# Looping over the feature chunks outermost in the first feed-forward step of each layer

## The chip, the cores and the metric

One core of one Trainium2 chip. The metric is the device time of one execution in microseconds (us); a kernel's time is the median of its runs. Engines run in parallel and each works through its own instructions in order: PE (TensorE, matmuls), ACT (ScalarE), DVE (VectorE), POOL (GpSimd), SP (issues the DMAs). They meet only at semaphores.

## What is computed

Two layers of a transformer-like trunk over 512 latent and 256 context tokens, width 1024. Only the feed-forward half of a layer matters here; in the second (last) layer the context tokens drop out of it.

```python
def swiglu(z, wg, wu, wd):
    return (jax.nn.silu(z @ wg) * (z @ wu)) @ wd
...
        mx = jnp.split(silu_c @ w_mod[l] + b_mod[l], 6, axis=-1)
        mc = jnp.split(silu_cc @ w_mod[l] + b_mod[l], 6, axis=-1)
...
        x = x + mx[5] * swiglu(modulate(rms_norm(x, norm2_g[l]), mx[3], mx[4]), w_gate[l], w_up[l], w_down[l])

        if not last:
...
            h = h + mc[5] * swiglu(modulate(rms_norm(h, norm2_g[l]), mc[3], mc[4]), w_gate[l], w_up[l], w_down[l])
```

The hidden width is 2816, the type is fp32 throughout.

## The kernel before

**Tiling.** Everything is kept transposed: features on the 128 partitions (8 chunks `k` of the 1024 features), tokens in the free dimension, 0 to 511 latent and 512 to 767 context. To keep fp32 precision each operand is split into a rounded part and a rest: `zh`/`zl` for the activations, `wh`/`wl` for the weights, and a product is three passes, `wh*zh + wh*zl + wl*zh`. `three_pass` (L1358) does that for one half panel: for each chunk `k`, three matmuls of 512 columns and, in layer 0, three of 256 for the context.

**The FFN.** It runs in 11 steps of 256 hidden units (`ffn_step`, L1604), each in two halves `h` of 128. A half has a gate accumulator in PSUM bank `3h`, an up accumulator in bank `3h + 1`, and both context parts in bank `3h + 2`. PE's order in a step: gate half 0, up half 0, gate half 1, up half 1, then the down projection of the step before (`down`, L1585). In layer 0 PE also computes one panel per step of layer 1's modulation row from `w_mod`: `ffn_mod(s, 0)` after up half 0 and `ffn_mod(s, 1)` after gate half 1, four matmuls for each of four quarters, from `wh_m`, `wl_m`, and then `mod_finish` (L1307) at the end of the step.

**The weights.** SP loads a panel into `raw`; ACT copies it, rounded, to `wh` (L487) as soon as the last user of that half is done (semaphores `use_a`, `use_b`, `use_m`, raised by PE); POOL subtracts to get `wl` (L382, semaphores `loA`, `loB`, `loM`, `loD`). `wh[0]` holds gate, `wh[1]` up, one panel each with two halves, `wh_m` the mod panel, `wh_d` down. ACT's order in a step: `gs` (the silu of the gate accumulator, half 0, after `use_b`), next gate half 0, next up half 0, in layer 0 two mod quarters, then `hh` (rounded hidden values, after DVE's product `hf`), and the same for half 1. POOL's order: `wl_d` x2, then for each half `wl` gate, `wl` up, `wl_m` x2. SP's order in a step of layer 0: gate, up, the two mod panels' halves (each waits for the previous `wl_m`), down (waits for the previous `wl_d`), then gate and up of the next step.

**The normalisation before the first step.** `norm(2l + 1)` makes the 8 chunks of z one after the other: DVE scales (`nxz`), ACT rounds (`zh`), POOL subtracts (`zl`; chunk 0 is DVE's). PE waits for chunk `k` by `z_wait`. After its last `zl`, POOL makes the first two `wl_m`, and ACT the two `wh_m` after its last `zh`.

**The first step before** is `ffn_step(0, 0, first=True)`: only its gate half 0 waits for the z chunks one by one.

Of the kernel before, what the change touches and what calls it, by code (L numbers as in the profile page):

```python
# [21 lines left out]
P = 128  # L22
D = 1024
KC = D // P
DEPTH = 2
SX = 512
SC = 256
# [50 lines left out]
def trunk(nc, x, c, ctx_in, c_ctx, w_mod, b_mod, norm1_g, norm2_g, w_in, ret_decay_f, ret_decay_b, ret_norm_g,  # L78
          attn_sink, cm_norm_g, cm_w_s, cm_b_s, w_out, w_gate, w_up, w_down, final_norm_g, consts, out):
    stack = ExitStack()  # L80
    with stack:
# [5 lines left out]
        def sem(name):  # L87
            if name not in sems:
                sems[name] = stack.enter_context(nc.semaphore(name))
            return sems[name]  # L90
# [14 lines left out]
        zh = sb("zh", [P, KC, NT], F32R)  # L105
        zl = sb("zl", [P, KC, NT], F32R)
        raw = [sb(f"raw{i}", [P, 2048]) for i in range(2)]
        wh = [sb(f"wh{i}", [P, 2, 1024], F32R) for i in range(2)]
        wl = [sb(f"wl{i}", [P, 2, 1024], F32R) for i in range(2)]
# [75 lines left out]
        ps = stack.enter_context(nc.psum_tensor("ps", [P, 8, 512], F32))  # L185

        def parts(l_or_w):
            return [(0, SX, 0)] + ([(SX, NT, 1)] if l_or_w else [])
# [12 lines left out]
        A_GATE = [a + 4 for a in A_OUT]  # L201
        N_MODB = 2 * NP_IN
        B_UP = [N_MODB, N_MODB + FSTEPS]

        J_IN, J_FFN = 4, 4 + NP_IN

        def z_wait(eng, u, k):

            if k in Z_DVE:
                eng.wait_ge(sem("z_dve"), len(Z_DVE) * u + Z_DVE.index(k) + 1)  # L210
            else:
                eng.wait_ge(sem("z_pool"), len(Z_POOL) * u + Z_POOL.index(k) + 1)
# [1081 lines left out]
        def _(pe):  # L1294
            MM, TR = nc.tensor.matmul, nc.tensor.transpose
# [11 lines left out]
            def mod_finish(J):  # L1307

                pe.wait_ge(sem("modrow_rdy"), J + 1)
                for i in range(4):  # L1310
                    last = MM(ps[:, MODCOLS[0], 256 + 2 * i:258 + 2 * i], modrow[0:4, P * i:P * i + P], sel, start=True, stop=True)
                last.then_inc(sem("mod_fin"), 1)
# [12 lines left out]
            for k in range(KC):  # L1325
                if k >= 2:
                    pe.wait_ge(sem("xt_evac"), k - 1)
                for t in range(6):
                    dst = ps[:, k % 2, P * t:P * t + P] if t < 4 else ps[:, 2 + k % 2, P * (t - 4):P * (t - 4) + P]
                    last = TR(dst, xin[:, t, P * k:P * k + P], eye)  # L1330
# [4 lines left out]
            for i in range(8):  # L1335
                last = TR(ps[:, 5 + i // 4, P * (i % 4):P * (i % 4) + P], cws[:, i, :], eye)
# [21 lines left out]
            def three_pass(wt_h, wt_l, h, dsts, ctx, norm_u=None):  # L1358

                for k in range(KC):  # L1360
                    w = slice(P * k, P * k + P)
                    if norm_u is not None:
                        z_wait(pe, norm_u, k)
                    for c0, c1, s in parts(ctx):
                        dst = dsts[s]
                        MM(dst, wt_h[:, h, w], zh[:, k, c0:c1], start=(k == 0), stop=False)  # L1366
                        MM(dst, wt_h[:, h, w], zl[:, k, c0:c1], start=False, stop=False)  # L1367
                        last = MM(dst, wt_l[:, h, w], zh[:, k, c0:c1], start=False, stop=(k == KC - 1))  # L1368
                return last
# [5 lines left out]
            for l in range(DEPTH):  # L1375
# [203 lines left out]
                def ffn_mod(s, h):  # L1579
                    for hh_ in range(2):  # L1580
                        pe.wait_ge(sem("loM"), 4 * s + 2 * h + hh_ + 1)
                        last = mod_half(2 * h + hh_, wh_m[:, hh_, :], wl_m[:, hh_, :])
                        last.then_inc(sem("use_m"), 1)

                def down(s, par, wd_h=wh_d, wd_l=wl_d):  # L1585
                    pe.wait_ge(sem(f"loD{l}"), 2 * s + 2)
                    pe.wait_ge(sem(f"h_rdy{l}"), 2 * s + 2)
                    start = type(s) is int and s == 0
                    for n in range(KC):
                        w = slice(P * n, P * n + P)  # L1590
                        for c0, c1, sc in parts(l == 0):

                            if sc == 0 and not (start and n == 0):
                                pe.wait_ge(sem(f"ev_d{l}"), KC * s + n)
                            if sc == 1 and not (start and n < 2):
                                pe.wait_ge(sem(f"ev_dc{l}"), KC * s + n - 1)
                            dst = ps[:, (0, 6)[n % 2], :] if sc == 0 else ps[:, (2, 7)[n % 2], 0:SC]
                            for k in range(2):
                                MM(dst, wd_h[:, k, w], hh[:, par, k, c0:c1], start=(k == 0), stop=False)  # L1599
                                MM(dst, wd_h[:, k, w], hl[:, par, k, c0:c1], start=False, stop=False)  # L1600
                                last = MM(dst, wd_l[:, k, w], hh[:, par, k, c0:c1], start=False, stop=(k == 1))  # L1601
                            last.then_inc(sem(f"dn{sc}_mm{l}"), 1)

                def ffn_step(s, par, first=False):  # L1604
                    a, b = A_GATE[l] + s, B_UP[l] + s
                    if not (type(s) is int and s < 2):

                        pe.wait_ge(sem(f"ev_d{l}"), KC * (s - 1))
                        if l == 0:
                            pe.wait_ge(sem("ev_dc0"), KC * (s - 1) - 1)  # L1610
                    for h in range(2):
                        pe.wait_ge(sem("loA"), 2 * a + h + 1)

                        pe.wait_ge(sem(f"ev_h{l}"), 2 * s + h) if not first else None
                        last = three_pass(wh[0], wl[0], h, (ps[:, 3 * h, :], ps[:, 3 * h + 2, 0:SC]), l == 0,
                                          2 * l + 1 if first and h == 0 else None)
                        last.then_inc(sem("use_a"), 1)
                        if l == 0 and h:
                            ffn_mod(s, 1)
                        pe.wait_ge(sem("loB"), 2 * (b - N_MODB) + h + 1)  # L1620
                        if l == 0 and h == 0 and not first:

                            pe.wait_ge(sem("modcol_rdy"), J_FFN + s)
                        last = three_pass(wh[1], wl[1], h, (ps[:, 3 * h + 1, :], ps[:, 3 * h + 2, SC:2 * SC]), l == 0)
                        last.then_inc(sem("use_b"), 1)
                        if l == 0 and h == 0:
                            if not first:

                                pe.wait_ge(sem("ev_d0"), KC * (s - 1) + 1)
                            ffn_mod(s, 0)  # L1630

                    pe.wait_ge(sem(f"ev_h{l}"), 2 * s + 2)
                    if l == 0:
                        mod_finish(J_FFN + s)
                    if not first:
                        down(s - 1, 1 - par)

                ffn_step(0, 0, first=True)
                ffn_step(1, 1)
                with pe.Fori(0, 4) as i:  # L1640
                    ffn_step(2 * i + 2, 0)
# [65 lines left out]
```

## Time and profile before

| | us |
|---|---|
| median of 3 runs | 2202.4 |
| lowest and highest run | 2200.58, 2208.09 |
| span of the profiled execution | 2204.4 |
| PE busy in it | 1927.6 (87%) |
| POOL busy | 665.9 (30%) |
| ACT busy | 629.6 (29%) |
| DVE busy | 874.0 (40%) |

The profiled execution lies 2.0 us above the median. The first FFN step of layer 0 runs from about 691 to 748 us of the span, that of layer 1 from about 1797 to 1829 us. In the rows further down, a time is the start from the beginning of the span, "idle before" stands in brackets with what ended it, and PEclk is the TensorE clock granted, as a share of 2.4 GHz.

### The profile page before, as it was taken

The numbers are of one execution on the slowest core, as the hardware profiler recorded it, in microseconds if no ns is written. First come the engines' busy times: TensorE is split into PE (matmuls) and PEld (weight loads), VectorE is DVE, ScalarE is ACT, GpSimd is POOL, SyncE is SP. The second block draws the span as 40 slices with busy tenths as digits, with TensorE's granted clock in tenths as the row PEclk, the third lists the DMA queues.
The fourth block names the chain that finished last, engine by engine and source line by source line (L and its number), as shares of the span: only waits on it lengthen the run. The fifth ranks groups of instructions, "written<-read, shape, count | busy, mean of one in ns | idle before, by whom it ended". The sixth has DMA issues, their size and how long they took to land.

```text
span 2204.4 us, 22301 instructions
## 1 busy us (share of the span) xinstructions
PE 1927.6 (87%) x8746; PEld 1443.3 (65%) x8746; DVE 874.0 (40%) x1238; ACT 629.6 (29%) x938; POOL 665.9 (30%) x288
## 2 busy tenths in 40 slices
PE   5589898978795989999999996987977869999997
PEld 4468772244484878888888884864134647877875
DVE  5653354255436122222222238125345352334235
ACT  6233332045413222222222212133135232212222
POOL 0521213000024444444444432233100145434440
PEclk8789995589996999999999997987579979999999
DMA  7233430000011322222222310121000131332321
GB/s 258 77 114 127 121 96 19 0 1 1 1 47 68 129 94 84 85 87 94 95 95 95 107 46 0 58 65 50 0 0 0 35 99 58 115 101 70 114 76 39
DMA packets 121902, 155.55 MB, mean 71 GB/s; under 512 B 20320, under 2 KB 89712, under 8 KB 121712
## 3 DMA queue, kind: packets, MB, share of 16 engines
q1 hardware_dynamic: 121840, 154.71, 22.2%
q8 instruction: 40, 0.66, 0.1%
q14 instruction: 22, 0.18, 0.0%
HBM read 152.60 MB, written 2.10 MB: 70 GB/s over the span
## 4 chain that ended last, share of the span: by engine, by line
PE 37%; issue 31%; DVE 12%; POOL 11%; ACT 5%; DMA 4%; SPq 1%; POOLq 0%; DVEq 0%; ACTq 0%
PE ps L1366 6%; PE ps L1367 6%; PE ps L1368 6%; POOL wl_m L382 5%; POOL wl L382 3%; PE ps L1468 3%; PE ps L1456 2%; PE ps L1599 2%; PE ps L1601 2%; PE ps L1600 2%; PE ps L1303 2%; DVE nxz L989 2%; POOL wl_d L382 2%; DVE wl L1004 1%; DMA raw<-in_w_in_dram 1%
## 5 line engine op out<-in xcount | busy, mean ns | idle before, releaser
L382 POOL TENSOR_TENSOR wl<-raw,wh 128x1024 fp32r<-128x1024 f32 x144 | 348.8, 2434 | 1200.6 <-ACT wh L487 1200.6
L1366 PE MATMUL ps<-zh,wh 128*128 128x512 f32 x1728 | 630.0, 365 | 72.9 <-DVE zl L974 38.0
L1367 PE MATMUL ps<-zl,wh 128*128 128x512 f32 x1728 | 625.1, 362 | 0.0
L1368 PE MATMUL ps<-zh,wl 128*128 128x512 f32 x1728 | 620.9, 359 | 0.0
L1366 PEld LDWEIGHTS ps<-zh,wh 128*128 128x128 f32 x1728 | 335.6, 194 | 141.2 <-issue 46.8
L1368 PEld LDWEIGHTS ps<-zh,wl 128*128 128x128 f32 x1728 | 334.5, 194 | 50.0
L1367 PEld LDWEIGHTS ps<-zl,wh 128*128 128x128 f32 x1728 | 336.0, 194 | 47.6
L487 ACT ACTIVATE wh<-raw 128x1024 fp32r<-128x1024 f32 (+1 forms) x186 | 196.3, 1086 | 420.9 <-DMA raw<-in_w_in_dram 147.9
L1254 DVE SCALAR_TENSOR_TENSOR xT<-ps,modcol,xT 128x512 f32<-128x512 f32 (+1 forms) x264 | 168.0, 661 | 97.8 <-PE ps L1601 94.3
L1235 DVE TENSOR_TENSOR hf<-gs,ps 128x512 f32<-128x512 f32 x66 | 37.6, 597 | 411.8 <-ACT gs L800 411.7
L1599 PE MATMUL ps<-hh,wh_d 128*128 128x512 f32 x480 | 173.5, 361 | 12.6 <-DVE xT L1254 12.5
L1600 PE MATMUL ps<-hl,wh_d 128*128 128x512 f32 x480 | 171.4, 357 | 0.0
L1601 PE MATMUL ps<-hh,wl_d 128*128 128x512 f32 x480 | 170.4, 355 | 0.0
L800 ACT ACTIVATE gs<-ps 128x512 f32<-128x512 f32 x44 | 26.4, 599 | 468.2 <-PE ps L1368 468.2
L1241 DVE TENSOR_TENSOR hl<-hf,hh 128x768 fp32r<-128x768 f32 (+1 forms) x44 | 92.5, 2102 | 124.0 <-ACT hh L487 124.0
L382 POOL TENSOR_TENSOR wl_d<-raw_d,wh_d 128x1024 fp32r<-128x1024 f32 x40 | 95.1, 2399 | 127.4 <-ACT wh_d L487 127.4
L382 POOL TENSOR_TENSOR wl_m<-raw_m,wh_m 128x1024 fp32r<-128x1024 f32 x44 | 119.4, 2732 | 0.0
L1468 PE MATMUL ps<-Pm,vtok 128*64 128x512 f32 (+1 forms) x112 | 100.9, 1011 | 12.1 <-DVE Pm L1116 12.1
L1599 PEld LDWEIGHTS ps<-hh,wh_d 128*128 128x128 f32 x480 | 91.1, 190 | 30.5 <-DVE xT L1254 16.9
L1456 PE MATMUL ps<-rq,rk 64*128 64x512 f32 (+1 forms) x112 | 102.7, 1022 | 0.0
L1601 PEld LDWEIGHTS ps<-hh,wl_d 128*128 128x128 f32 x480 | 90.8, 189 | 13.6
L1600 PEld LDWEIGHTS ps<-hl,wh_d 128*128 128x128 f32 x480 | 91.2, 190 | 12.5
(204 smaller groups left out, 2095.0 us busy)
## 6 DMA issues: line engine op xcount, KB each, us to landing
raw<-in_w_mod_dram SPq DMA_DIRECT2D x24, 1024.0 KB, 5.3
raw<-in_w_gate_dram SPq DMA_DIRECT2D x22, 1024.0 KB, 7.1
raw<-in_w_up_dram SPq DMA_DIRECT2D x22, 1024.0 KB, 9.5
raw_m<-in_w_mod_dram SPq DMA_DIRECT2D x22, 1024.0 KB, 5.2
raw_d<-in_w_down_dram SPq DMA_DIRECT2D x20, 1024.0 KB, 5.1
raw<-in_w_in_dram SPq DMA_DIRECT2D x14, 1024.0 KB, 6.8
raw<-in_w_out_dram SPq DMA_DIRECT2D x32, 256.0 KB, 4.4
raw<-in_w_in_dram SPq DMA_DIRECT2D x16, 256.0 KB, 4.6
```

Of the source, the lines that this page charges most:

```text
L382: nc.gpsimd.tensor_tensor(dst, src, hi.bitcast(F32), ALU.subtract).then_inc(sem(done), 1)
L487: return nc.scalar.activation(dst, src, ACT.Copy)
L1241: V.tensor_tensor(hl[:, par, h, 0:W], hf[:, 0:W], hh[:, par, h, 0:W].bitcast(F32), ALU.subtract).then_inc(sem(f"h_rdy{l}"), 1)
L1254: last = V.scalar_tensor_tensor(xT[:, n, c0:c1], src, modcol[:, 48 * l + 40 + n, sc:sc + 1], xT[:, n, c0:c1], ALU.mult, ALU.add)
L1366: MM(dst, wt_h[:, h, w], zh[:, k, c0:c1], start=(k == 0), stop=False)
L1367: MM(dst, wt_h[:, h, w], zl[:, k, c0:c1], start=False, stop=False)
L1368: last = MM(dst, wt_l[:, h, w], zh[:, k, c0:c1], start=False, stop=(k == KC - 1))
L1456: MM(ps[:, j % 3, 0:q.stop - q.start], rk[b:b + 64, r, P * c:P * c + P], rq[b:b + 64, r, q], start=True, stop=True).then_inc(sem(f"ret_sc{ ...
L1468: last = MM(ps[b:b + 64, 5 + s, 0:n], vtok[:, c, HD * h:HD * h + HD], Pm[:, j % 3, 0:n], start=first, stop=(c == 5))
L1599: MM(dst, wd_h[:, k, w], hh[:, par, k, c0:c1], start=(k == 0), stop=False)
L1600: MM(dst, wd_h[:, k, w], hl[:, par, k, c0:c1], start=False, stop=False)
L1601: last = MM(dst, wd_l[:, k, w], hh[:, par, k, c0:c1], start=False, stop=(k == 1))
```

## The change

`ffn_first` replaces `ffn_step(0, 0, first=True)`. Its outer loop runs over the chunks `k`; inside it, halves and gate or up; four accumulators (with the context six regions) are open at once. The context parts of gate and up share a bank, so only the first matmul into it has the start flag. The semaphores `use_a` and `use_b` are raised by the last chunk only. Both parts of mod panel 0 leave the middle of the step: `ffn_mod(0, 0)` stands ahead of the loop, `ffn_mod(0, 1)` behind it. ACT, DVE, POOL and SP keep their code.

```diff
--- before.py
+++ after.py
@@ -1601,7 +1601,35 @@
                                 last = MM(dst, wd_l[:, k, w], hh[:, par, k, c0:c1], start=False, stop=(k == 1))
                             last.then_inc(sem(f"dn{sc}_mm{l}"), 1)
 
-                def ffn_step(s, par, first=False):
+                def ffn_first():
+
+                    a, b = A_GATE[l], B_UP[l]
+                    if l == 0:
+                        ffn_mod(0, 0)
+                    pe.wait_ge(sem("loA"), 2 * a + 2)
+                    pe.wait_ge(sem("loB"), 2 * (b - N_MODB) + 2)
+                    for k in range(KC):
+                        w = slice(P * k, P * k + P)
+                        z_wait(pe, 2 * l + 1, k)
+                        for h in range(2):
+                            for up in range(2):
+                                wt_h, wt_l = wh[up][:, h, w], wl[up][:, h, w]
+                                for c0, c1, sc in parts(l == 0):
+                                    dst = ps[:, 3 * h + up, :] if sc == 0 else ps[:, 3 * h + 2, SC * up:SC * up + SC]
+                                    opens = k == 0 and not (sc and up)
+                                    MM(dst, wt_h, zh[:, k, c0:c1], start=opens, stop=False, skip_group_check=True)
+                                    MM(dst, wt_h, zl[:, k, c0:c1], start=False, stop=False, skip_group_check=True)
+                                    last = MM(dst, wt_l, zh[:, k, c0:c1], start=False, stop=(k == KC - 1), skip_group_check=True)
+                                if k == KC - 1:
+                                    last.then_inc(sem(("use_a", "use_b")[up]), 1)
+                    if l == 0:
+                        ffn_mod(0, 1)
+
+                    pe.wait_ge(sem(f"ev_h{l}"), 2)
+                    if l == 0:
+                        mod_finish(J_FFN)
+
+                def ffn_step(s, par):
                     a, b = A_GATE[l] + s, B_UP[l] + s
                     if not (type(s) is int and s < 2):
 
@@ -1611,31 +1639,28 @@
                     for h in range(2):
                         pe.wait_ge(sem("loA"), 2 * a + h + 1)
 
-                        pe.wait_ge(sem(f"ev_h{l}"), 2 * s + h) if not first else None
-                        last = three_pass(wh[0], wl[0], h, (ps[:, 3 * h, :], ps[:, 3 * h + 2, 0:SC]), l == 0,
-                                          2 * l + 1 if first and h == 0 else None)
+                        pe.wait_ge(sem(f"ev_h{l}"), 2 * s + h)
+                        last = three_pass(wh[0], wl[0], h, (ps[:, 3 * h, :], ps[:, 3 * h + 2, 0:SC]), l == 0)
                         last.then_inc(sem("use_a"), 1)
                         if l == 0 and h:
                             ffn_mod(s, 1)
                         pe.wait_ge(sem("loB"), 2 * (b - N_MODB) + h + 1)
-                        if l == 0 and h == 0 and not first:
+                        if l == 0 and h == 0:
 
                             pe.wait_ge(sem("modcol_rdy"), J_FFN + s)
                         last = three_pass(wh[1], wl[1], h, (ps[:, 3 * h + 1, :], ps[:, 3 * h + 2, SC:2 * SC]), l == 0)
                         last.then_inc(sem("use_b"), 1)
                         if l == 0 and h == 0:
-                            if not first:
-
-                                pe.wait_ge(sem("ev_d0"), KC * (s - 1) + 1)
+
+                            pe.wait_ge(sem("ev_d0"), KC * (s - 1) + 1)
                             ffn_mod(s, 0)
 
                     pe.wait_ge(sem(f"ev_h{l}"), 2 * s + 2)
                     if l == 0:
                         mod_finish(J_FFN + s)
-                    if not first:
-                        down(s - 1, 1 - par)
-
-                ffn_step(0, 0, first=True)
+                    down(s - 1, 1 - par)
+
+                ffn_first()
                 ffn_step(1, 1)
                 with pe.Fori(0, 4) as i:
                     ffn_step(2 * i + 2, 0)
```

What PE has in its queue in layer 0 behind the normalisation's statistics (L1319), before: the gate panel's matmuls (`wh0`, `wl0`) at once.

```order
L1319 MATMUL ps<-nacc,consts_sb 128x256
L1366 MATMUL ps<-zh,wh0 128x512 [waits z_dve,loA]
L1367 MATMUL ps<-zl,wh0 128x512
L1368 MATMUL ps<-zh,wl0 128x512
L1366 MATMUL ps<-zh,wh0 128x256
L1367 MATMUL ps<-zl,wh0 128x256
L1368 MATMUL ps<-zh,wl0 128x256
```

And in the changed kernel: the mod panel first, then gate and up (`wh1`, `wl1`) of one chunk in turn.

```order
L1319 MATMUL ps<-nacc,consts_sb 128x256
L1303 MATMUL ps<-wh_m,c4 128x512 [waits loM]
L1303 MATMUL ps<-wl_m,c4 128x512
L1303 MATMUL ps<-wh_m,c4 128x512
L1303 MATMUL ps<-wl_m,c4 128x512
L1303 MATMUL ps<-wh_m,c4 128x512 [waits loM]
L1303 MATMUL ps<-wl_m,c4 128x512
L1303 MATMUL ps<-wh_m,c4 128x512
L1303 MATMUL ps<-wl_m,c4 128x512
L1620 MATMUL ps<-zh,wh0 128x512 [waits z_dve,loB,loA]
L1621 MATMUL ps<-zl,wh0 128x512
L1622 MATMUL ps<-zh,wl0 128x512
```

Eight matmuls that wait for `loM` now stand between the statistics and the first matmul of the FFN.

The end of the same step, before: the last up matmuls, then `mod_finish` (L1311) and the next step.

```order
L1367 MATMUL ps<-zl,wh1 128x512
L1368 MATMUL ps<-zh,wl1 128x512
L1366 MATMUL ps<-zh,wh1 128x256
L1367 MATMUL ps<-zl,wh1 128x256
L1368 MATMUL ps<-zh,wl1 128x256
L1311 MATMUL ps<-consts_sb,modrow 128x2 [waits modrow_rdy,ev_h0]
L1311 MATMUL ps<-consts_sb,modrow 128x2 x3
L1366 MATMUL ps<-zh,wh0 128x512 [waits ev_h0,loA]
```

And in the changed kernel:

```order
L1622 MATMUL ps<-zh,wl1 128x256
L1303 MATMUL ps<-wh_m,c4 128x512 [waits loM]
L1303 MATMUL ps<-wl_m,c4 128x512
L1303 MATMUL ps<-wh_m,c4 128x512
L1303 MATMUL ps<-wl_m,c4 128x512
L1303 MATMUL ps<-wh_m,c4 128x512 [waits loM]
L1303 MATMUL ps<-wl_m,c4 128x512
L1303 MATMUL ps<-wh_m,c4 128x512
L1303 MATMUL ps<-wl_m,c4 128x512
L1311 MATMUL ps<-consts_sb,modrow 128x2 [waits modrow_rdy,ev_h0]
L1311 MATMUL ps<-consts_sb,modrow 128x2 x3
L1366 MATMUL ps<-zh,wh0 128x512 [waits ev_h0,loA]
```

`ffn_mod(0, 1)`, which stood between gate half 1 and up half 1, now stands behind all of the step's matmuls and ahead of `mod_finish` and the next step.

## Rows read from the trace of the kernel before

**Rows 1.** Stages of layer 0: us, busy PE, PEld, DVE, ACT, POOL, then PEclk.

```profile
700.00:717.00 17.00, 12.78 (x35) 9.87 (x36) 10.38 (x12) 6.55 (x7) 12.31 (x7) 0.50 0.00 1
717.00:726.00 9.00, 9.00 (x52) 7.84 (x52) 0.56 (x1) 0.87 (x2) 0.97 (x1) 0.99 0.78 256
814.00:871.00 57.00, 55.88 (x317) 48.42 (x316) 16.47 (x26) 12.86 (x17) 25.19 (x10) 1.00 0.29 93
```

**Rows 2.** PE timeline, layer 0, step 0: start, us, engine, line, what, idle before.

```profile
691.09 0.76 PE L1366 MATMUL ps<-zh,wh 128*128 128x512 f32 x1 [11.26 <-DVE zl L974]
...
738.33 0.50 PE L1303 MATMUL ps<-wh_m,c 128*128 128x512 f32 x1 [1.83 <-POOL wl_m L382]
...
747.85 1.05 PE L1311 MATMUL ps<-consts_sb,modrow 4*128 4x2 f32 x8
```

**Rows 3.** PE timeline, layer 0, step 1.

```profile
781.95 0.79 PE L1303 MATMUL ps<-wh_m,c 128*128 128x512 f32 x1 [5.81 <-POOL wl_m L382]
...
784.98 0.80 PE L1303 MATMUL ps<-wh_m,c 128*128 128x512 f32 x1 [0.96 <-POOL wl_m L382]
...
786.85 0.63 PE L1366 MATMUL ps<-zh,wh 128*128 128x512 f32 x1
...
796.24 0.94 PE L1311 MATMUL ps<-consts_sb,modrow 4*128 4x2 f32 x7
```

**Rows 4.** POOL timeline, layer 0, steps 0 and 1.

```profile
713.27 4.71 POOL L382 TENSOR_TENSOR wl_m<-raw_m,wh_m 128x1024 fp32r<-128x1024 f32 x2
...
749.85 4.80 POOL L382 TENSOR_TENSOR wl<-raw,wh 128x1024 fp32r<-128x1024 f32 x2 [11.58 <-ACT wh L487]
754.59 5.47 POOL L382 TENSOR_TENSOR wl_m<-raw_m,wh_m 128x1024 fp32r<-128x1024 f32 x2
760.03 4.74 POOL L382 TENSOR_TENSOR wl_d<-raw_d,wh_d 128x1024 fp32r<-128x1024 f32 x2
...
779.57 5.36 POOL L382 TENSOR_TENSOR wl_m<-raw_m,wh_m 128x1024 fp32r<-128x1024 f32 x2
```

**Rows 5.** ACT timeline, layer 0, steps 0 and 1.

```profile
726.46 1.06 ACT L487 ACTIVATE wh<-raw 128x1024 fp32r<-128x1024 f32 x1 [0.77 <-DMA raw<-in_w_gate_dram]
...
747.96 0.60 ACT L800 ACTIVATE gs<-ps 128x512 f32<-128x512 f32 x1 [14.91 <-PE ps L1368]
...
773.17 1.06 ACT L487 ACTIVATE wh<-raw 128x1024 fp32r<-128x1024 f32 x1 [6.37 <-DMA raw<-in_w_gate_dram]
```

**Rows 6.** DVE timeline, layer 0, step 0.

```profile
739.62 0.68 DVE L861 COPY modrow<-ps 4x512 f32<-4x512 f32 x1 [3.56 <-PE ps L1303]
```

**Rows 7.** The page's DMA issues: what, queue, count, KB each, us to landing.

```profile
raw_m<-in_w_mod_dram SPq DMA_DIRECT2D x22, 1024.0 KB, 5.2
```

**Rows 8.** ACT timeline, layer 1, steps 0 and 1.

```profile
1818.25 0.60 ACT L800 ACTIVATE gs<-ps 128x512 f32<-128x512 f32 x1 [7.87 <-PE ps L1368]
...
1829.13 0.60 ACT L800 ACTIVATE gs<-ps 128x512 f32<-128x512 f32 x1 [7.87 <-PE ps L1368]
...
1851.92 1.06 ACT L487 ACTIVATE wh<-raw 128x1024 fp32r<-128x1024 f32 x1 [1.88 <-DMA raw<-in_w_up_dram]
```

**Rows 9.** A stage of layer 1 (as rows 1), and PE's timeline there.

```profile
1797.00:1813.00 16.00, 13.07 (x26) 7.38 (x27) 11.21 (x14) 5.06 (x7) 10.51 (x7) 0.51 0.09 31
...
1796.81 0.76 PE L1366 MATMUL ps<-zh,wh 128*128 128x512 f32 x1 [9.46 <-DVE zl L974]
...
1828.93 0.39 PE L1366 MATMUL ps<-zh,wh 128*128 128x512 f32 x1
...
1857.41 0.80 PE L1599 MATMUL ps<-hh,wh_d 128*128 128x512 f32 x1 [3.83 <-DVE xT L1254]
```

**Rows 10.** POOL timeline, layer 1, steps 0 and 1.

```profile
1808.03 2.74 POOL L382 TENSOR_TENSOR zl<-nxz,zh 128x512 fp32r<-128x512 f32 x2 [1.09 <-ACT zh L487]
1819.87 5.20 POOL L382 TENSOR_TENSOR wl<-raw,wh 128x1024 fp32r<-128x1024 f32 x2 [9.10 <-ACT wh L487]
...
1835.93 4.75 POOL L382 TENSOR_TENSOR wl_d<-raw_d,wh_d 128x1024 fp32r<-128x1024 f32 x2
```

## The prediction

> **What bounds the kernel now.** I read the granted clock and PE's busy time by stage first, then PE's timeline in the first feed-forward (FFN) step of each layer, then ACT and POOL, which prepare the weights. In the steady FFN steps of layer 0, PE is busy 55.9 of 57.0 us at full clock: PE sets the pace and whatever arrives late there is not won back [rows 1]. The first step is different. PE starts it at 691.09 and follows the normalisation, which gives one of the eight z chunks about every 3.3 us; until 717 the clock is 0.50 of full (the 1.2 GHz level), afterwards 0.99 (2.4 GHz) [rows 1, 2]. That waiting is what the change wants to fill. But PE also waits in steps 0 and 1 for the converted `w_mod` panels (`wl_m`), which come out of a chain ACT, POOL, DMA, ACT, POOL: at 738.33 for 1.83 us, at 781.95 for 5.81 us, at 784.98 for 0.96 us [rows 2, 3].
>
> **The change, layer 0: the front.** The new order puts the first half of modulation panel 0 (`ffn_mod(0, 0)`) ahead of all FFN matmuls. PE is in order, so all 192 matmuls queue behind `loM`. POOL computes these two `wl_m` halves after its last z chunk, at 713.27, 4.71 us for both: they end at 715.6 and 718.0 [rows 4]. By then every z chunk is there, so nothing overlaps with the normalisation in layer 0; the quarter that used to run beside it (from 691.09) now runs behind it. The second group of four matmuls takes 1.87 us at the low clock (784.98 to 786.85) [rows 3]: 718.0 + 1.9 = 719.9. One half of gate or of up is 8 chunks of 6 matmuls (three passes of 512 and of 256 columns), 48, and takes 8.4 us at full clock (738.33 to 747.85, less 1.1 for the four mod matmuls at its front) [rows 2], four of them 33.6. PE was idle before 715.6, so the clock is low at first; before, it rose 3.7 us after the last z wait ended (713.3 to 717) [rows 1, 4]; between 2 and 4 us at half speed cost 1 to 2, I take 1.5. The step's matmuls end at 719.9 + 33.6 + 1.5 = **755.0**, where before they ended at 747.85 with both mod groups done [rows 2].
>
> **Layer 0: the tail.** All four accumulators close in the last chunk. So the buffers `wh0` and `wh1`, whose first halves were free at about 725 before (ACT had done its `gs` and stood idle 0.77 us until 726.46, for the gate load) [rows 5], are freed 12 matmuls (2.1 us) before the end: `gs` starts at 753.0. Behind it on ACT and POOL come the next gate half, the next up half, then two `wl_m` halves. This sequence is in the trace undisturbed: `gs` at 747.96, `wl` x2 at 749.85, `wl_m` x2 at 754.59 for 5.47, so the first `wl_m` is 9.4 and the second 12.1 us after `gs` [rows 4, 5]. Now 762.4 and 765.1. PE has nothing else: the second half of panel 0 stands next, and step 1 behind it. It idles 755.0 to 762.4 and so loses the clock (after the 5.81 us wait before 781.95 the matmuls were at the low clock: four in the 1.87 us above) [rows 3]. Mod matmuls end at 767.0; the row copy on DVE (0.68) and the four small matmuls (1.05 at full clock, I take 1.5) [rows 2, 6] put step 1 at **769.3**, against 748.9 before: +20.4.
>
> **Layer 0: what is given back in step 1.** Before, step 1 lost 6.8 us to `wl_m` itself [rows 3]. In the new order: `wl_m` at 765.1 lets SP load the next mod panel, 5.2 us and 0.3 for the issue [rows 7], 770.6; one ACT half 1.1, two `wl_m` 5.4, 777.1; two `wl_d` 4.7, 781.8. That was 764.77 before (760.03 + 4.74) [rows 4], so +17.0. From there gate and up for step 2 are loaded (landing 8.4 us later, 773.17) [rows 5] and the `wl_m` pair that ended at 784.93 (779.57 + 5.36) ends at 801.9 [rows 4]. PE by itself: 769.3 + 16.8 + 1.2 for the low clock + 1.9 for mod + 8.4 = 797.6. So it waits, less than before, ends the mod matmuls at 802.9 and, now warm, the last up half at 811.3 against 796.24 [rows 3]: **+15.1**. From there every wait in the trace is tied to PE's own releases and the shift stays. Bounds: +10.7 if the `wl_m` chain is not the later one (797.6 + 1.0 + 8.4 = 807.0), +18 if the clock falls again in the waits and the last half takes the 9.4 us it took before [rows 3].
>
> **Layer 1.** There are no mod panels and only 512-column matmuls, 0.227 us apart at full clock (48 of them between the two `gs` at 1818.25 and 1829.13) [rows 8]. The z chunks come at 1796.8 to 1810.8, one per 2.0 us [rows 9, 10]; one chunk of four accumulators is 12 matmuls, 5.1 us at the low clock and 2.7 at full, so PE never waits again after the first. The granted clock was 0.51 over 1797 to 1813 [rows 9], while PE had gaps; without them I let it rise 4.4 us after the start, which costs 2.2. End: 1796.8 + 0.1 + 21.8 + 2.2 = **1820.9**, against 1828.93 [rows 9]: -8.0. The tail gives part back: `gs` comes 6 matmuls before the end, 1819.75; `wl` starts 1.62 later (1818.25 to 1819.87) [rows 8, 10], its first half is ready at 1823.9, and PE restarts there, -5.0. POOL then runs two pairs (5.2 each) and `wl_d` (4.75) without a pause and ends at 1836.5, against 1835.93 + 4.75 = 1840.68 [rows 10]: -4.2. This one counts: gate and up of step 2 are loaded behind `wl_d` (ACT gets up at 1851.92) [rows 8], ACT converts them ahead of `hh`, DVE needs `hh` ahead of the evacuations, and so PE sat 3.83 us inside the first down projection, until 1857.41 [rows 9]. That restart moves to 1853.2; PE is there at 1848.4 and waits. **-4.2**, bounds -6.5 (the clock rises at once and POOL follows) and 0.
>
> The rule that speaks against this nest: the Trainium skill, TensorE: Matmul & The Clock Gate, section "Loop structure matters more than you think", calls it good to loop over output tiles outside and K tiles inside, because matmuls then stay back to back. Here that nest is the kernel before, and its clock was 0.50 and 0.51 during the normalisation [rows 1, 9]: with the moving operand arriving late, the trace speaks for K outside.
>
> **Sum.** +15.1 - 4.2 = +10.9 on the span of 2204.4, so 2215.3 in a profile; the median of the runs is 2.0 lower than the profiled time, so **2213.3**. All PE, ACT, POOL and DMA work is the same in number; only order changes, which is worth nothing outside the two places.
>
> **Rivals.** (a) Not slower: the DMA chain hides layer 0. Before, ACT's first conversion at 726.46 waited for the gate load, not for PE [rows 5]; if that load still decided, layer 0 would be 0 and the time 2198.2. It decides only while `gs` starts before about 725; I have 753, so 0.05. (b) Layer 0 bound by PE alone, +10.7: 2208.9; needs `wl_m` before 798 instead of 802. 0.10. (c) Layer 1 gives nothing: if PE reaches the down projection 9 us later than I have it, by a low clock over the whole of step 1: 2217.5, 0.08. (d) The mod panel does not hold the front, the change does in both layers what it says: PE starts at 691.1, ends near 727, `wl_d` at 755.0 instead of 764.8, -9.8: 2188.4. Against it stands the place of `loM` in the order. 0.03. (e) The clock stays at 1.2 GHz through layer 1's loop: 96 matmuls of 0.427 end at 1837.8, `wl_d` +11.4: 2228.9, 0.02. This last one is how the page's rule above would come out.
>
> **How the numbers follow.** The forecast has 0.70. The range, 2208 to 2219, takes in (b) and (c) and the bounds of the tails. The 0.02 left is for what I have not seen. A measurement here tells 0.3%, 6.6 us, from no change: faster 0.03 is (d); same 0.10 is (a) and half of (b); slower 0.87 is the rest.
>
> **What would show it.** Layer 0: no FFN matmul before 718; an idle PE of 7 us or so after the first step, ended by `wl_m`; a shorter wait in the middle of step 1; PE's end of step 1 about 15 us later. Layer 1: no gap between the z chunks after the first, clock up before 1803 on the old axis, a PE wait of 3 us for `wl` after the step, and the wait inside the first down projection still there. I am wrong if layer 0's first matmuls start near 691, if the tail costs less than 5 us in layer 0, or if layer 1's lead of 8 us survives whole.

## Result and the profile after

| | before | changed |
|---|---|---|
| median of 8 runs, us | 2202.38 | 2215.48 |
| lowest and highest | 2200.58, 2208.74 | 2212.2, 2223.81 |
| span of the profiled execution | 2204.4 | 2222.0 |

The ratio of the times is 1.0054, with a 95% interval of 1.0036 to 1.0072; the medians are 13.1 us apart. The forecast was 2213.3. The profiled execution of the changed kernel took 2223.7 us (its span is 2222.0), 8.3 above its median: it is one of the three longest of the eight, which had a mean clock of 0.890 to 0.893, while the five others had 0.897 or 0.898.

Both kernels compute the sum of squares of each normalisation with the matmuls of L1319, the same in both. They cut the span into stretches that can be compared. PE's timeline, kernel before:

```profile
676.90 2.93 PE L1319 MATMUL ps<-nacc,consts_sb 128*128 128x512 f32 x4 [5.54 <-DVE nacc L890]
...
1341.79 2.93 PE L1319 MATMUL ps<-nacc,consts_sb 128*128 128x512 f32 x4 [2.66 <-DVE nacc L890]
...
1785.28 2.07 PE L1319 MATMUL ps<-nacc,consts_sb 128*128 128x512 f32 x2 [5.21 <-DVE nacc L890]
...
2186.73 1.13 PE L1319 MATMUL ps<-nacc,consts_sb 128*128 128x512 f32 x2 [2.29 <-DVE nacc L890]
```

And the changed kernel:

```profile
679.79 2.93 PE L1319 MATMUL ps<-nacc,consts_sb 128*128 128x512 f32 x4 [5.54 <-DVE nacc L890]
...
1361.95 1.84 PE L1319 MATMUL ps<-nacc,consts_sb 128*128 128x512 f32 x4 [2.66 <-DVE nacc L890]
...
1808.79 2.08 PE L1319 MATMUL ps<-nacc,consts_sb 128*128 128x512 f32 x2 [6.45 <-DVE nacc L890]
...
2204.20 1.13 PE L1319 MATMUL ps<-nacc,consts_sb 128*128 128x512 f32 x2 [2.29 <-DVE nacc L890]
```

The stretch with layer 0's FFN (first mark to second) was 664.9 and is 682.2 (+17.3); the one with layer 1's FFN (third to fourth) was 401.5 and is 395.4 (-6.0). That is 11.3. The rest of the 17.6 between the two spans, 6.3, lies where the code is the same: 2.9 ahead of the first mark, 3.4 in layer 1's attention part. More of it below. In the rows, "cold" means the 1.2 GHz level, at which the first matmul after a wait shows 0.8 us, and "warm" the 2.4 GHz level, at which it shows 0.5.

**Layer 0.** PE, the first step and the next; columns as in [rows 2]. It answers to [rows 2, 3].

```profile
718.50 0.80 PE L1303 MATMUL ps<-wh_m,c 128*128 128x512 f32 x1 [35.78 <-POOL wl_m L382]
...
720.83 0.79 PE L1303 MATMUL ps<-wh_m,c 128*128 128x512 f32 x1 [0.25 <-POOL wl_m L382]
...
764.97 0.79 PE L1303 MATMUL ps<-wh_m,c 128*128 128x512 f32 x1 [7.57 <-POOL wl_m L382]
...
767.30 0.80 PE L1303 MATMUL ps<-wh_m,c 128*128 128x512 f32 x1 [0.25 <-POOL wl_m L382]
...
770.27 1.02 PE L1311 MATMUL ps<-consts_sb,modrow 4*128 4x2 f32 x8 [0.93 <-DVE modrow L861]
...
801.26 0.50 PE L1303 MATMUL ps<-wh_m,c 128*128 128x512 f32 x1 [1.22 <-POOL wl_m L382]
...
804.28 0.80 PE L1303 MATMUL ps<-wh_m,c 128*128 128x512 f32 x1 [1.83 <-POOL wl_m L382]
...
816.45 1.05 PE L1311 MATMUL ps<-consts_sb,modrow 4*128 4x2 f32 x8
```

PE idles 35.78 us until the first `wl_m` half, at 718.50; no FFN matmul comes earlier. Behind the step it idles 7.57 us, again for `wl_m`; step 1 starts behind the small matmuls at 770.27, about 771.3. In step 1 the two waits for `wl_m` are 1.22 and 1.83 us, where they were 5.81 and 0.96. The ends of step 1 (816.45 and 796.24) lie 136.7 and 119.3 us behind the first mark: +17.3, which is the whole shift of the stretch. POOL, the same time (it answers to [rows 4]):

```profile
716.11 4.67 POOL L382 TENSOR_TENSOR wl_m<-raw_m,wh_m 128x1024 fp32r<-128x1024 f32 x2
...
761.86 5.38 POOL L382 TENSOR_TENSOR wl_m<-raw_m,wh_m 128x1024 fp32r<-128x1024 f32 x2
767.21 4.68 POOL L382 TENSOR_TENSOR wl<-raw,wh 128x1024 fp32r<-128x1024 f32 x2
773.86 5.45 POOL L382 TENSOR_TENSOR wl_m<-raw_m,wh_m 128x1024 fp32r<-128x1024 f32 x2 [1.97 <-ACT wh_m L487]
779.28 4.75 POOL L382 TENSOR_TENSOR wl_d<-raw_d,wh_d 128x1024 fp32r<-128x1024 f32 x2
...
798.83 5.40 POOL L382 TENSOR_TENSOR wl_m<-raw_m,wh_m 128x1024 fp32r<-128x1024 f32 x2
```

Its `wl_m` pairs end at 720.78, 767.24, 779.31 and 804.23. The late start of this chain shows on ACT, which idled until the loop's end released the buffers:

```profile
755.35 0.60 ACT L800 ACTIVATE gs<-ps 128x512 f32<-128x512 f32 x1 [37.96 <-PE ps L1622]
```

**Layer 1.** PE and then POOL, in one window each, answering to [rows 9, 10]:

```profile
1820.32 0.76 PE L1620 MATMUL ps<-zh,wh 128*128 128x512 f32 x1 [9.46 <-DVE zl L974]
...
1846.80 0.47 PE L1366 MATMUL ps<-zh,wh 128*128 128x512 f32 x1 [2.76 <-POOL wl L382]
...
1875.94 0.50 PE L1599 MATMUL ps<-hh,wh_d 128*128 128x512 f32 x1 [2.79 <-DVE xT L1254]
```

```profile
1844.34 10.31 POOL L382 TENSOR_TENSOR wl<-raw,wh 128x1024 fp32r<-128x1024 f32 x4 [9.94 <-ACT wh L487]
1854.62 4.72 POOL L382 TENSOR_TENSOR wl_d<-raw_d,wh_d 128x1024 fp32r<-128x1024 f32 x2
```

From the mark at 1808.79, step 1 starts 38.0 us later (before 43.7), and PE goes on inside the first down projection 67.2 us later (before 72.1). After the first z chunk PE has no wait in the loop.

And the stages (columns: us, busy PE, PEld, DVE, ACT, POOL, PEclk, DMA, GB/s):

```profile
803.00:810.00 7.00, 5.72 (x17) 4.78 (x17) 0.68 (x1) 0.00 (x0) 1.23 (x1) 0.52 0.46 150
1824.00:1844.00 20.00, 20.00 (x89) 16.22 (x87) 8.52 (x11) 5.13 (x8) 8.22 (x6) 1.00 0.00 0
1847.00:1851.00 4.00, 4.00 (x12) 3.15 (x12) 2.32 (x3) 3.53 (x5) 4.00 (x2) 0.60 0.01 4
1875.00:1882.00 7.00, 5.90 (x24) 4.54 (x25) 5.00 (x7) 0.63 (x1) 4.10 (x2) 1.00 0.01 2
```

The clock was up again at 1824, 3.7 us after the start (it was 0.51 over this place before). It was 0.52 at 803 to 810: the matmuls at 801.26 were still warm (0.50), those at 804.28, behind the second of the two short waits of layer 0's step 1, were cold (0.80). It also fell behind the 2.76 us wait ahead of step 1 in layer 1 (0.60 over 1847 to 1851), but not behind the one in the down projection.

### The profile page after: what moved, and what is told of

It is laid out like the page before. It is cut to its first block, busy times and chain, and to the rows that moved or that the text cites. A ratio compares the mean times of both kernels' runs of the same rounds, so it can differ in the third digit from the quotient of the medians.

```text
span 2222.0 us, 22301 instructions
## 1 busy us (share of the span) xinstructions
PE 1927.5 (87%) x8746; PEld 1443.7 (65%) x8746; DVE 869.1 (39%) x1238; ACT 629.0 (28%) x938; POOL 669.8 (30%) x288
## 4 chain that ended last, share of the span: by engine, by line
PE 38%; issue 31%; DVE 11%; POOL 10%; ACT 5%; DMA 3%; SPq 1%; POOLq 0%; DVEq 0%; ACTq 0%
PE ps L1366 6%; PE ps L1367 6%; PE ps L1368 6%; POOL wl_m L382 5%; POOL wl L382 3%; PE ps L1468 3%; PE ps L1456 2%; PE ps L1599 2%; PE ps L1600 2%; PE ps L1601 2%; PE ps L1303 2%; POOL wl_d L382 1%; DVE nxz L989 1%; DVE wl L1004 1%; DMA raw<-in_w_in_dram 1%
## 5 line engine op out<-in xcount | busy, mean ns | idle before, releaser
L1366 PE MATMUL ps<-zh,wh 128*128 128x512 f32 x1632 | 590.5, 362 | 46.3 <-DVE zl L974 19.9
L1367 PE MATMUL ps<-zl,wh 128*128 128x512 f32 x1632 | 588.2, 360 | 0.0
L1368 PE MATMUL ps<-zh,wl 128*128 128x512 f32 x1632 | 583.9, 358 | 0.0
L1366 PEld LDWEIGHTS ps<-zh,wh 128*128 128x128 f32 x1632 | 315.6, 193 | 103.3 <-issue 29.7
L1368 PEld LDWEIGHTS ps<-zh,wl 128*128 128x128 f32 x1632 | 314.7, 193 | 46.8
L1367 PEld LDWEIGHTS ps<-zl,wh 128*128 128x128 f32 x1632 | 315.7, 193 | 45.0
L1600 PE MATMUL ps<-hl,wh_d 128*128 128x512 f32 x480 | 171.0, 356 | 0.0
L382 POOL TENSOR_TENSOR wl_m<-raw_m,wh_m 128x1024 fp32r<-128x1024 f32 x44 | 119.3, 2730 | 2.0 <-ACT wh_m L487 2.0
L1599 PEld LDWEIGHTS ps<-hh,wh_d 128*128 128x128 f32 x480 | 90.7, 189 | 30.0 <-DVE xT L1254 16.4
L1601 PEld LDWEIGHTS ps<-hh,wl_d 128*128 128x128 f32 x480 | 90.5, 189 | 13.4
```

Source lines behind the costliest of these rows:

```text
L382: nc.gpsimd.tensor_tensor(dst, src, hi.bitcast(F32), ALU.subtract).then_inc(sem(done), 1)
```

## Experiments

Every kernel was timed against the kernel before on the same chip; these are three other chips than that of the first 8 runs. On them the kernel before had a median of 2209 to 2211 us and a spread of 2202 to 2220, wider than in those 8. So each row has the ratio and, from its profile, the two stretches between the marks above. The kernel before has one profile, the one shown above. The whole times named in the expectations start from the 2202.4 of those first runs, so they are compared as differences.

| kernel | median, before beside it | ratio, 95% interval | layer 0 stretch | layer 1 stretch |
|---|---|---|---|---|
| before | | | 664.9 | 401.5 |
| changed | 2215.5, 2202.4 | 1.0054 (1.0036 to 1.0072) | 682.2 | 395.4 |
| e1, layer 1 only | 2208.1, 2209.0 | 1.0001 (0.9987 to 1.0016) | 664.5 | 397.8 |
| e9, the same again | 2207.1, 2209.1 | 0.9993 (0.9978 to 1.0008) | 664.6 | 397.5 |
| e2, layer 0 only | 2226.3, 2209.0 | 1.0079 (1.0056 to 1.0102) | 681.0 | 402.1 |
| e8, mod in front alone | 2222.3, 2211.0 | 1.0049 (1.0030 to 1.0069) | 675.4 | 402.2 |
| e10, two open, mod in front | 2216.0, 2209.1 | 1.0028 (1.0010 to 1.0046) | 675.2 | 395.9 |
| e3, mod behind the loop | 2193.6, 2209.0 | 0.9938 (0.9917 to 0.9959) | 660.1 | 398.0 |
| e4, two open | 2207.7, 2209.0 | 0.9993 (0.9978 to 1.0009) | 667.9 | 396.9 |
| e7, loads alone | 2200.9, 2211.0 | 0.9955 (0.9937 to 0.9973) | 660.1 | 397.6 |
| e6, four open, mod behind, loads | 2186.7, 2211.0 | 0.9889 (0.9870 to 0.9908) | 652.1 | 393.5 |
| e5, two open, loads | 2184.5, 2211.0 | 0.9892 (0.9872 to 0.9912) | 651.6 | 391.5 |

How well a stretch repeats can be read from kernels that have the same code in it. Layer 0 agrees to 0.4 us with the old step (before, e1, e9) and to 1.2 with the changed one (changed, e2). Layer 1 agrees to 0.7 with the old step (before, e2, e8), but with the changed one it spreads from 395.4 to 398.0 (changed, e1, e9, e3).

### Which layer pays (e1, e9, e2)

```diff
-                ffn_first()
+                (ffn_first if l else ffn_first_old)()
```

`ffn_first_old` is the old first step. e2 has the two names the other way round.

> The new first step in layer 1 only; layer 0 keeps the old order. Theory (layer 0 pays, layer 1 earns): 4 to 6 us faster than before, 2196.4 to 2198.4, and the stretch of layer 1 from the normalisation's statistics to those of the last normalisation 6.0 us shorter, as in the changed kernel. Rival (four open accumulators cost by themselves, in matmul rate or late release, in either layer): no gain or a loss, 2202 or more.

> The new first step in layer 0 only; layer 1 keeps the old order. Theory: 15 to 18 us slower than before, 2217.4 to 2220.4, which with the layer 1 kernel adds up to the whole change. Rival (the two places are not independent, part of the loss is a different clock pattern in stages that were not changed): less than 12 us, or a sum of the two that misses the whole change by more than 4 us.

> The layer 1 only kernel once more, since its whole time was level with before (interval from 0.13% faster to 0.16% slower) while its profile showed the stretch of layer 1 3.6 us shorter. Theory (layer 1 gains 3.5 to 6 us, hidden in the spread of the runs): stretch of layer 1 395 to 398 us against 401.5, median 2 to 6 us below before. Rival (no gain): stretch 400 or more in this profile, or a median above before's.

Layer 0 alone is 16.1 us longer in its stretch and 17.3 in the median, as expected. Layer 1 alone is 3.6 to 3.9 us shorter in its stretch, twice, less than the 6.0 I had expected of e1. In the whole time it is 0.9 and 1.9 below before, less than the 4 to 6 I had said for e1 and the 2 to 6 for e9, and neither interval tells it from zero. The two medians add up to +16.4, against the +13.1 of the whole change, inside the 4 us that I had set. That layer 1 gains is shown by the stretches; that the kernel is faster by it is not.

### What layer 0 pays for (e8, e10)

e8 is the kernel before with only the front changed:

```diff
                     a, b = A_GATE[l] + s, B_UP[l] + s
+                    if first and l == 0:
+                        ffn_mod(0, 0)
...
-                            ffn_mod(s, 0)
+                                ffn_mod(s, 0)
```

> The kernel before with one edit: the first part of mod panel 0 stands ahead of gate half 0 in step 0 of layer 0; the loops keep their old order and weights are released half by half. Theory: the front alone costs layer 0 10 to 12 us, so that some 5 of the 16 to 17 of the changed kernel are the late release. Rival (the late release is the larger part): 5 or less.

e10 also has the mod part in front, but its chunk loop opens two accumulators, gate and up of half 0; half 1 follows in the old order, with `ffn_mod(0, 1)` between its gate and its up. (The changed kernel keeps eight PSUM regions open in six banks in layer 0, four latent and four context ones; the six named with the change are the banks.)

```diff
-                        for h in range(2):
-                            for up in range(2):
+                        for up in range(2):
...
+                    three_pass(wh[0], wl[0], 1, (ps[:, 3, :], ps[:, 5, 0:SC]), l == 0).then_inc(sem("use_a"), 1)
+                    if l == 0:
+                        ffn_mod(0, 1)
+                    three_pass(wh[1], wl[1], 1, (ps[:, 4, :], ps[:, 5, SC:2 * SC]), l == 0).then_inc(sem("use_b"), 1)
```

> Mod panel's first part in front in layer 0, as in the changed kernel, but only two accumulators open in the loop, so that the weight buffers are released half by half. Theory (layer 0 pays 10 to 11 for the front and 5 to 7 for the late release): stretch of layer 0 674 to 677 us, between before's 664.9 and the changed kernel's 682.2, and no idle PE of 7 us behind the step. Rival (the front alone explains all): 680 or more.

PE in e10:

```profile
718.45 0.79 PE L1303 MATMUL ps<-wh_m,c 128*128 128x512 f32 x1 [35.78 <-POOL wl_m L382]
...
749.73 0.50 PE L1303 MATMUL ps<-wh_m,c 128*128 128x512 f32 x1 [1.39 <-POOL wl_m L382]
...
752.05 0.50 PE L1303 MATMUL ps<-wh_m,c 128*128 128x512 f32 x1 [1.13 <-POOL wl_m L382]
...
761.56 1.05 PE L1311 MATMUL ps<-consts_sb,modrow 4*128 4x2 f32 x8
```

The wait in front is the same 35.78 us, but the 7.57 us behind the step are gone; 1.39 and 1.13 are left inside it. Both kernels have a layer 0 stretch of 675, 10.3 to 10.5 above before, as I had expected of both. With the old loops and with a two-accumulator loop it is the same, so that is the price of the front. The changed kernel and e2 are 5.6 to 7.0 above it. That is the price of the late release of the weight buffers together with the place of `ffn_mod(0, 1)`: e10 also puts it back between gate half 1 and up half 1, while in the changed kernel nothing else stands ahead of it that PE could do meanwhile. No run changes one of the two without the other.

### The mod part behind the loop (e3)

```diff
-                    if l == 0:
-                        ffn_mod(0, 0)
                     pe.wait_ge(sem("loA"), 2 * a + 2)
...
                     if l == 0:
+                        ffn_mod(0, 0)
                         ffn_mod(0, 1)
```

> The changed kernel with one edit: the first part of mod panel 0 stands behind the chunk loop of layer 0, ahead of the second part, not in front of the loop. Theory (the wait for wl_m at the front is what costs): PE starts at about 691, ends the loop near 728, the wl_m wait stays where it was before (738), layer 0 is 9 to 11 us faster than before, together with layer 1 14 to 17 us: 2185 to 2188. Rival (the late release of the weight buffers by four open accumulators is what costs): still at or above the time of before, 2202 to 2210.

The loop overlaps now, and the kernel beats the one before by 0.62%, 15.4 us in the medians, inside the 14 to 17 I had given for the two layers. But in the profile layer 0 gains 4.8 us, half of what I expected, and layer 1 3.5. The profiled execution of e3 took 2207.0, 13.4 above its median, so where the other 7 us of the medians lie is open. PE in e3:

```profile
741.42 0.79 PE L1303 MATMUL ps<-wh_m,c 128*128 128x512 f32 x1 [7.29 <-POOL wl_m L382]
...
744.45 0.79 PE L1303 MATMUL ps<-wh_m,c 128*128 128x512 f32 x1 [0.96 <-POOL wl_m L382]
...
747.46 1.83 PE L1311 MATMUL ps<-consts_sb,modrow 4*128 4x2 f32 x8 [0.93 <-DVE modrow L861]
...
781.02 0.79 PE L1303 MATMUL ps<-wh_m,c 128*128 128x512 f32 x1 [2.98 <-POOL wl_m L382]
```

PE was through with its part of the step 7.29 us before `wl_m` and then ran cold: the small matmuls at 747.46 take 1.83 instead of 1.05 [rows 2]. In step 1 a wait of 2.98 us is still there, where it was 5.81 [rows 3]. The gain in front ended in a longer wait for a chain that had not moved as far.

### Two accumulators in place of four (e4)

The loop of e10, with `ffn_mod(0, 0)` in its old place between the halves.

> Chunk loop outermost over gate half 0 and up half 0 only (two accumulators, three regions with the shared context bank), then mod, gate half 1, mod, up half 1 in the old order; in both layers. Theory: layer 1 gains 5.8 (half 0 ends 1.4 us after the last z chunk and weights are released early), layer 0 gains about nothing, since step 0 then ends by wl_m, whose chain starts at the gate load that lands at 726: 2195 to 2198. Rival (only the overlap with the normalisation counts): layer 0 gains 9 too, 2187 or so.

PE's wait, the stage around it, and ACT, all of e4:

```profile
738.12 0.79 PE L1303 MATMUL ps<-wh_m,c 128*128 128x512 f32 x1 [7.50 <-POOL wl_m L382]
```

```profile
733.00:747.00 14.00, 7.93 (x21) 6.08 (x22) 3.57 (x2) 2.96 (x4) 7.68 (x3) 0.52 0.24 76
```

```profile
718.75 0.60 ACT L800 ACTIVATE gs<-ps 128x512 f32<-128x512 f32 x1 [1.27 <-PE ps L1618]
...
729.35 1.06 ACT L487 ACTIVATE wh<-raw 128x1024 fp32r<-128x1024 f32 x1 [9.73 <-DMA raw<-in_w_gate_dram]
```

Layer 1 gains 4.6 (I had 5.8). Layer 0 gets worse by 3.0, where I had said that it gains about nothing. The whole time is level with before: 1.3 us below it, where I had 4 to 7. Half 0 is done early (`gs` at 718.75), ACT then stands idle 9.73 us until 729.35 for the gate load, PE 7.50 us until 738.12 for what comes of it, and in that longer idle the clock falls: 0.52 over 733 to 747. The kernel before had arrived at the same wait later:

```profile
735.30 0.50 PE L1303 MATMUL ps<-wh_m,c 128*128 128x512 f32 x1 [0.32 <-POOL wl_m L382]
```

```profile
739.00:748.00 9.00, 9.00 (x53) 7.73 (x51) 0.68 (x1) 0.04 (x1) 0.00 (x0) 1.00 0.36 118
```

Both get this `wl_m` half 58.4 us behind the first mark (738.12 and 735.30). Before, PE had waited 0.32 us for it and went on at full clock; e4 had waited 7.50 and went on cold. The engine that arrived earlier at the same wait came out later: the small matmuls at the end of the step start 173.7 us behind the first mark in e4, 171.0 before.

### The loads (e7, e5, e6)

SP loads gate and up of step 1 ahead of the second mod half, and in each later step gate and up of the next one ahead of down, and the next step's first mod half behind down:

```diff
                 if l == 0:
                     load_modm(0, 0, first=True)
+                load_ffn(l, 1)
+                if l == 0:
                     load_modm(0, 1)
+                    load_modm(1, 0)
                 with sp.Fori(1, FSTEPS - 1) as s:
-                    load_ffn(l, s)
                     if l == 0:
-                        load_modm(s, 0)
                         load_modm(s, 1)
+                    load_ffn(l, s + 1)
                     load_down(l, s)
-                load_ffn(l, FSTEPS - 1)
+                    if l == 0:
+                        load_modm(s + 1, 0)
                 if l == 0:
-                    load_modm(FSTEPS - 1, 0)
                     load_modm(FSTEPS - 1, 1)
```

> The kernel before with SP's loads in the new order and nothing else. Theory: layer 0 loses its waits at 738 and 782, 9 to 12 us, layer 1 the wait in the first down projection and the low clock behind it, 4 to 6; 13 to 18 us faster in all. Rival (these waits are off what counts): within 3 us of before.

> Two accumulators open in the first step (gate and up of half 0), and SP's loads in another order: gate and up of step s+1 are issued ahead of down s and, for step 1, ahead of the second mod half. Theory (what keeps layer 0 from its gain is the chain wl_m, load, convert, wl_m): the 7.5 us wait for wl_m in step 0 and the 5.8 us wait in step 1 go, layer 0 is 16 to 20 us shorter than before, layer 1 9 to 12: 26 to 32 us faster than before. Rival (the chain is bound by ACT and POOL, not by the loads): no more than 8 us faster.

> Four accumulators open, both parts of mod panel 0 behind the loop, and SP's loads in the new order. Theory: layer 0 is 14 to 18 us shorter than before, layer 1 8 to 11, 22 to 28 us faster in all; behind the step PE still waits 5 to 9 us for wl_m, since four accumulators release the weights late, so it comes out 2 to 6 us behind the kernel with two accumulators. Rival (late release costs nothing once the loads are early): level with it.

e7 is the kernel before with these loads, e5 is e4 with them, e6 is e3 with them. Alone they bring 0.45%, 10.1 us in the medians, less than the 13 to 18 I had given: layer 0 gains 4.8 (I had 9 to 12), layer 1 3.9 (4 to 6). PE in e7, step 0 and step 1:

```profile
739.39 0.50 PE L1305 MATMUL ps<-wh_m,c 128*128 128x512 f32 x1 [1.07 <-POOL wl_m L384]
...
778.53 0.50 PE L1305 MATMUL ps<-wh_m,c 128*128 128x512 f32 x1 [1.35 <-POOL wl_m L384]
...
781.56 0.80 PE L1305 MATMUL ps<-wh_m,c 128*128 128x512 f32 x1 [1.83 <-POOL wl_m L384]
```

The waits were 1.83, 5.81 and 0.96 [rows 2, 3] and are 1.07, 1.35 and 1.83: 4.4 less, close to the 4.8 of the stretch. I had let them go to nothing. They still end by POOL's `wl_m`; what holds that up now was not followed further.

With the new loads, the overlap pays: e5 and e6 are 1.1% faster than the kernel before, 26.5 and 24.3 us. Layer 0 is 13.3 and 12.8 shorter (I had 16 to 20 and 14 to 18), layer 1 10.0 and 8.0, as expected. It is more than the sum of the parts: in layer 0, e4 alone is 3.0 longer and e7 4.8 shorter, both together 13.3 shorter. PE in e5, step 0 and step 1:

```profile
733.89 0.50 PE L1305 MATMUL ps<-wh_m,c 128*128 128x512 f32 x1 [1.22 <-POOL wl_m L384]
...
773.13 0.50 PE L1305 MATMUL ps<-wh_m,c 128*128 128x512 f32 x1 [1.42 <-POOL wl_m L384]
...
776.15 0.80 PE L1305 MATMUL ps<-wh_m,c 128*128 128x512 f32 x1 [1.83 <-POOL wl_m L384]
```

The 7.50 us wait of e4 is 1.22. What is left in step 1 (1.42 and 1.83) is what e7 has there. And in e6:

```profile
735.77 0.79 PE L1305 MATMUL ps<-wh_m,c 128*128 128x512 f32 x1 [5.81 <-POOL wl_m L384]
...
1815.54 0.47 PE L1368 MATMUL ps<-zh,wh 128*128 128x512 f32 x1 [2.75 <-POOL wl L384]
```

Four accumulators still leave 5.81 us of idle PE behind the step in layer 0, as expected, and 2.75 in layer 1 for the first `wl` of step 1. But whole times of e5 and e6 are level, and so are their layer 0 stretches, to 0.5 us: my rival, that late release costs nothing once the loads are early, came true there. The trace says why. In layer 0 the two-accumulator loop of e5 has less to do per chunk than the chunks take to come, and waits in step 0 for 0.50, 0.90, 0.90, 0.93 and 0.65 us on `zl` and for 1.16 and 1.22 on `wl_m`, 6.3 in all; e6 has no gap in its loop and waits 5.81 and 0.25 behind it. The 2.0 us between them in layer 1 are less than the spread of that stretch from profile to profile.

## Why the prediction was right

**The front of layer 0** came out as worked out. On the old axis (the new first mark is 2.9 later) the first mod matmul is at 715.6, the eighth ends near 719.8, the step's matmuls end near 754.5, against 755.0. e8 gives the price of the front as 10.5.

**The tail** too: `gs` at 755.35, which is 752.5 on the old axis, against 753.0; `wl_m` ready 9.6 and 11.9 us later, against 9.4 and 12.1; step 1 starts at 768.4, against 769.3. e10, which releases half by half and has `ffn_mod(0, 1)` in its old place, is 5.6 to 7.0 shorter in layer 0 than e2 and the changed kernel, not the 5 I then gave this in e8's expectation.

**What step 1 gives back** was the term that was mis-sized. I had +15.1 for layer 0; it is +17.3. The `wl_m` pair ended at 801.3 on the old axis, against 801.9, so the chain was right. But I let PE go through the last waits warm. It waited 1.22 and 1.83 us, and the matmuls behind the second wait were cold; the last up half, from 806.15 (804.28 and four matmuls at the low clock, 1.87) to 816.45, took 10.3 us instead of 8.4. This is the case that I had as the upper bound, +18. By the prediction's own terms that bound is +17: the `wl_m` pair is 17.0 later, and behind it the four matmuls and the last half take what they took before. The lower bound, rival (b), counts four mod matmuls where eight are left at 797.6; with eight (1.8 us) it is about +11.6 and 2209.7 in place of +10.7 and 2208.9.

**Layer 1** was right in its mechanism: -4.2 forecast, -6.0 in this profile, and -3.5 to -3.9 in e1, e9 and e3, which have the same code there. The loop ended near 1844.0, 35.2 us behind the mark, against 35.6; PE restarted 5.6 us earlier (I had 5.0), `wl_d` ended at 1859.34, 50.6 behind the mark against 55.4 before, -4.8 (I had -4.2), and the wait in the down projection was still there, 2.79 us. The rest is clock: before, the first matmul behind that wait took 0.80 us [rows 9] and the clock was 0.76 over 1857 to 1864; in the changed kernel it took 0.50, and the clock stayed at 1.00 over 1875 to 1882. That was luck of this execution. In e1, e9 and e3, in this order, the same wait was followed by the low clock:

```profile
1852.57 0.50 PE L1599 MATMUL ps<-hh,wh_d 128*128 128x512 f32 x1 [4.41 <-DVE xT L1254]
```

```profile
1854.92 0.79 PE L1599 MATMUL ps<-hh,wh_d 128*128 128x512 f32 x1 [4.55 <-DVE xT L1254]
```

```profile
1855.95 0.79 PE L1599 MATMUL ps<-hh,wh_d 128*128 128x512 f32 x1 [2.96 <-DVE xT L1254]
```

In e1 only the first matmuls are warm; the clock was 0.66 over 1852 to 1857. The lead of 8 us at the end of the loop did not survive, as the sum had it.

**Where luck helped.** The two misses have opposite signs: layer 0 cost 2.2 us more than forecast and layer 1 gave 1.8 more, so that +10.9 and +11.3 lie closer together than either part. And the medians moved by 13.1, of which the two stretches account for 11.3.

**The rivals.** (a), the load hides layer 0, falls with the 17.3 us by which that stretch is longer. (d), the front does not hold, falls with the 35.78 us wait. (b), PE alone bounds step 1, falls with the 1.22 and 1.83 us waits that ended by `wl_m`. (c), layer 1 gives nothing, falls by its stretch (395 to 398 in all six profiles with an overlapping loop in layer 1 and the old loads, against 401 to 402 in the three without). (e), the clock stays low in layer 1's loop, falls with the clock of 1.00 over 1824 to 1844. The nest that the Trainium skill, TensorE: Matmul & The Clock Gate, section "Loop structure matters more than you think", calls good is not the warmer one here, where the moving operand arrives chunk by chunk: it had 0.51 over 1797 to 1813 [rows 9]. As the bad case that section of the Trainium skill shows only a nest with a DMA wait before every matmul; it does not speak of K outside, and that its rule would come out as (e) was my reading.

**What stays open.** The profile is 17.6 us longer and the two places explain 11.3. The median moved by 13.1. The stretches that no kernel changed vary too: ahead of the first mark from 676.3 to 683.6, and layer 1's attention part from 443.5 to 448.8, over the twelve profiles. The mean clock does not explain the first of these: over the first 676 us it was 0.83 in e1, which reached the mark at 676.3, and 0.84 in e2, which reached it at 683.6. Whether the change shifts these stretches on average, or they differ only by chance in one profile each, the runs do not settle.

## What to carry to other kernels

An in-order engine overlaps only up to the first wait in its queue. When a loop is reordered to fill a wait, list everything that is moved in front of it and ask when its operands are made; here one small side job put 192 matmuls behind the end of the very phase they were to overlap. The more accumulators are open at once, the later all their weight buffers come free, and the next step's conversion starts from zero. Fewer accumulators are not better for that alone: each chunk then carries less work, and gaps come back into the loop. Two were 5.6 to 7.0 us better than four in layer 0 with the mod part in front (e10), 7.8 worse with the old loads (e4 against e3, where the mod parts stand in different places too), and level with the new ones (e5, e6). And a gain in front is kept only if the chain that ends the next wait moves as well. In e3 and e4 it did not move far enough, and PE, early at the wait, lost its clock there.

## What the runs showed of the hardware

A longer wait can cost more than its length. In e4, PE reached its wait earlier, idled 7.50 us instead of 0.32, and had 0.52 of the clock over 14 us; the step ended later than before, although the operand came at the same time. And the length of a wait alone does not tell whether the clock falls: two waits of 1.22 and 1.83 us, 3 us apart, had the clock at 0.52 over 803 to 810 in the changed kernel, while one of 1.83 us before and one of 2.79 us in layer 1 were not followed by a low spell. The plainest case is the wait of 2.75 to 2.76 us for `wl` ahead of step 1 in layer 1, with the same matmuls around it: behind it the clock was 0.60 over 4 us in the changed kernel and 0.61 in e3, but 1.00 over more than 6 us in e1 and e9.

The same code does not take the same time in every execution. That ahead of the FFN, from the start to the first mark, took 676.3 us in one profile and 683.6 in another, and the whole kernel before spread over 2202 to 2220 us on the three other chips. A gain of 4 us in one place is seen in the stretch and is lost in the whole time.
